# Three groups of small TensorE products per attention head placed beside other small groups, and the weight-sum jobs of GpSimd in another order

## What is computed

```python
def diff_attn_core(q, k, v, q_pos, k_pos, lam):
    s = jnp.einsum('bqhmd,bkhmd->bhmqk', q, k).astype(jnp.float32) * (DIFF_HEAD_DIM ** -0.5)
    visible = (k_pos[None, :] // CHUNK) <= (q_pos[:, None] // CHUNK)
    p = jax.nn.softmax(jnp.where(visible, s, NEG), axis=-1)
    a = p[:, :, 0] - lam * p[:, :, 1]
    return jnp.einsum('bhqk,bkhe->bqhe', a.astype(v.dtype), v)

def finish_layer(x, a, b, ga, gb, w_a, w_b, w_o, g1, b1, w_up, w_down, g2, b2):
    mix = (ga * (a @ w_a) + gb * (b @ w_b)) @ w_o
    x = layer_norm(ALPHA * x + mix, g1, b1)
    h = jnp.square(jax.nn.relu(x @ w_up)) @ w_down
    return layer_norm(ALPHA * x + h, g2, b2)
```

## Time and profile before

| | us |
|---|---|
| median of 3 runs | 2132.62 (2132.21 to 2136.03) |
| profiled execution, time | 2132.67 |
| profiled execution, span of the core | 2130.9 |
| PE busy | 2116.2 |
| DVE / ACT busy | 1472.1 / 1230.6 |
| HBM over the span | 228 GB/s |

### The profile page before, as it was taken

One profiled execution on the slowest core, in us unless ns is written; L12 is line 12 of the kernel. 1 busy time (PEld: TensorE's weight loads), 2 busy tenths in 40 slices (PEclk: granted clock), 3 DMA queues, 4 the chain that ended last, 5 costly groups with the idle time before them and its releaser, 6 DMA issues.

```text
span 2130.9 us, 38215 instructions
## 1 busy us (share of the span) xinstructions
PE 2116.2 (99%) x15004; PEld 1935.2 (91%) x15004; DVE 1472.1 (69%) x2336; ACT 1230.6 (58%) x2493; POOL 64.6 (3%) x100
## 2 busy tenths in 40 slices
PE   9999999999999999999999999999999999999998
PEld 8998889999989898989889888899999898989897
DVE  6857777766879356665667577786778793566656
ACT  4457776696535356656234577766965353556561
POOL 1000000001000000000001000000110001000000
PEclk9999999999999999999999999999999999999999
DMA  7887562487861855454368765524778527544541
GB/s 251 237 291 257 204 219 107 146 250 218 222 228 50 237 158 171 146 168 139 109 188 240 279 251 211 211 79 156 244 206 246 204 73 224 166 165 154 168 149 70
DMA packets 100867, 399.27 MB, mean 187 GB/s; under 512 B 15273, under 2 KB 16937, under 8 KB 87601
## 3 DMA queue, kind: packets, MB, share of 16 engines
q1 hardware_dynamic: 67904, 191.55, 26.4%
q0 software_dynamic: 7936, 92.28, 17.1%
q10 hardware_dynamic: 24848, 112.99, 14.8%
HBM read 367.42 MB, written 118.23 MB: 228 GB/s over the span
## 4 chain that ended last, share of the span: by engine, by line
PE 96%; DMA 2%; ACT 1%; DVE 1%; issue 0%; ACTq 0%; DVEq 0%
PE PS L828 9%; PE PS L830 9%; PE PS L829 9%; PE PS L1049 6%; PE PS L1051 6%; PE PS L1050 6%; PE PS L917 5%; PE PS L919 5%; PE PS L918 5%; PE PS L863 4%; PE PS L862 4%; PE PS L861 4%; PE PS L987 3%; PE PS L988 3%; PE PS L989 3%; PE PS L1177 2%
## 5 line engine op out<-in xcount | busy, mean ns | idle before, releaser
L828 PE MATMUL PS<-xt_hi,w_hi 128*128 128x320 f32 x1184 | 382.3, 323 | 0.2
L830 PE MATMUL PS<-xt_hi,w_lo 128*128 128x320 f32 x1184 | 365.9, 309 | 0.0
L829 PE MATMUL PS<-xt_lo,w_hi 128*128 128x320 f32 x1184 | 365.7, 309 | 0.0
L2541 DVE TENSOR_TENSOR w_lo<-w_raw,w_hi 128x1024 fp32r<-128x1024 f32 x146 | 177.5, 1222 | 151.0 <-ACT w_hi L1579 149.4
L2548 DVE TENSOR_TENSOR w_lo<-w_raw,w_hi 128x1024 fp32r<-128x1024 f32 (+1 forms) x176 | 199.3, 1138 | 114.8 <-ACT w_hi L1595 114.5
L1579 ACT ACTIVATE w_hi<-w_raw 128x1024 fp32r<-128x1024 f32 x146 | 153.6, 1059 | 178.5 <-PE PS L1051 152.6
L828 PEld LDWEIGHTS PS<-xt_hi,w_hi 128*128 128x128 f32 x1184 | 222.8, 188 | 5.4 <-issue 4.3
L829 PEld LDWEIGHTS PS<-xt_lo,w_hi 128*128 128x128 f32 x1184 | 223.0, 188 | 0.1
L830 PEld LDWEIGHTS PS<-xt_hi,w_lo 128*128 128x128 f32 x1184 | 222.3, 188 | 0.0
L1595 ACT ACTIVATE w_hi<-w_raw 128x1024 fp32r<-128x1024 f32 (+1 forms) x176 | 172.2, 984 | 86.1 <-PE PS L989 66.3
L1049 PE MATMUL PS<-w_hi,act_a_hi 128*128 128x512 f32 x480 | 187.9, 391 | 2.3 <-DVE rows L3007 2.3
(11 more groups left out here) (391 smaller groups left out, 5095.0 us busy)
## 6 DMA issues: line engine op xcount, KB each, us to landing
w_raw<-in_weights SPq DMA_DIRECT2D x186, 512.0 KB, 4.8
kc<-in_k_cache ACTq DMA_DIRECT2D x32, 1024.0 KB, 7.7
vc<-in_v_cache ACTq DMA_DIRECT2D x16, 2048.0 KB, 8.7
w_raw<-up_sums SPq DMA_DIRECT2D x112, 256.0 KB, 2.9
up_sums<-in_up_blocks POOLq DMA_DIRECT2D x24, 1024.0 KB, 9.0
w_raw<-in_up_blocks SPq DMA_DIRECT2D x84, 256.0 KB, 2.8
down_sums<-in_down_blocks POOLq DMA_DIRECT2D x16, 1024.0 KB, 11.3
w_raw<-in_down_blocks SPq DMA_DIRECT2D x32, 512.0 KB, 3.4
```

Source lines behind the costliest of these rows:

```text
L828: mm(out, wh, hi[:, k, c], start=(k == 0), stop=False)
L829: mm(out, wh, lo[:, k, c], start=False, stop=False)
L830: last = mm(out, wl, hi[:, k, c], start=False, stop=(k == KT - 1))
L2541: v.tensor_tensor(w_lo[slot][:], raw[:, raw_of(s, n)[0], :], w_hi[slot][:].bitcast(F32), ALU.subtract)\
```

## The change

```diff
 def sum_jobs():
 
-    return [(l, kind, part) for l in range(DEPTH) for part in range(FF_PARTS) for kind in ("up", "down")
-            if kind == "up" or part in BLOCK_PARTS]
+    order = (("up", 1), ("down", 1), ("up", 0), ("up", 2), ("down", 2), ("up", 3))
+    return [(l, kind, part) for l in range(DEPTH) for kind, part in order]
...
             for j, (l, kind, part) in enumerate(SUM_JOBS):
-                if (kind, part) == ("up", 0):
+                if (kind, part) == ("up", 1):
                     pool.wait_ge(w_ready[0], nth(l, AT_V) + 1)
-                elif (kind, part) == ("down", 1):
+                elif (kind, part) == ("up", 0):
                     pool.wait_ge(swa_cache_loaded, 32 * (l + 1))
...
-                tile(0, 0, None if first else {(0, 1): lambda: unit_transpose(l, h - 1, (3,)),
+                tile(0, 0, None if first else {(0, 1): lambda: (unit_product(l, h - 1, (2,)),
+                                                                unit_transpose(l, h - 1, (3,))),
                                                (0, 6): lambda: mean_squares(n - 1)})
...
                 if not first:
                     output_transposes(l, h - 1, 7)
-                tile(1, 0, {(0, 2): lambda: dec_transposes(l, h, 0), (0, 5): lambda: dec_transposes(l, h, 1)})
+                dec_transposes(l, h, 0)
+                tile(1, 0, {(0, 4): lambda: dec_transposes(l, h, 1)})
                 dec_products(l, h)
                 unit_score(l, h, p, (3,))
                 unit_transpose(l, h, (0, 1))
-                tile(1, 1, {(1, 4): lambda: dec_map_sum(l, h),
-                            (1, 5): lambda: (unit_product(l, h, (0, 1)), unit_transpose(l, h, (2,)))})
-                unit_product(l, h, (2,))
+                tile(1, 1, {(1, 5): lambda: (unit_product(l, h, (0, 1)), dec_map_sum(l, h),
+                                             unit_transpose(l, h, (2,)))})
 
             def last_head_end(l):
-                early_gate(l, 2, 0, {(0, 1): lambda: unit_transpose(l, HEADS - 1, (3,)),
+                early_gate(l, 2, 0, {(0, 1): lambda: (unit_product(l, HEADS - 1, (2,)),
+                                                      unit_transpose(l, HEADS - 1, (3,))),
                                      (0, 6): lambda: mean_squares(l * HEADS + HEADS - 1)})
```

## The result

| | before | after |
|---|---|---|
| median of 4 runs, us | 2132.41 (2131.74 to 2136.03) | 2153.49 (2150.72 to 2155.11) |
| profiled execution, time / span, us | 2132.67 / 2130.9 | 2153.41 / 2151.6 |
| granted TensorE clock over the span | 0.999 | 0.995 |

The ratio is 1.0094 (95% interval 1.0075 to 1.0114): slower, by 21 us. I had forecast +9.6 us, 2142.3, with 2150 as the high end. The direction was right, the size was not, and the time lies outside the range.

A forecast was written before the change was run, and what follows sets the result against it. PE was taken as the bound, busy 2116.2 of 2130.9 us. The terms -1.3 + 8.4 + 1.3 + 3.5 - 2.3 = +9.6 us, on 2132.67, gave 2142.3 us, range 2137 to 2150.

The forecast's parts named there:

- The stall: Heads 1 to 7, both layers: fifth decode transpose waits for ACT's copy out of bank 7; 14 x 0.60 = +8.4 us.
- The rival in which the wait does not bite: Heads: ACT copies sooner or the fifth transpose is not held; +1.2, 2133.9 us, no change; chance 0.06.
- Grouping: PE in all 16 heads: putting small groups together saves 0.08 us a head, -1.3 us, between 0 and -2.
- The end of the last head: Early gate 2: unit 2's six products no longer cover the wait for gate 1's copy; +0.66 a layer, +1.3 us.
- The O stage: Waits before L1049 vanish because POOL's last transfer goes out some 15 us earlier; -2.3 us, between -2.3 and 0.
- The keys: Head 0's cached-key loads delayed by POOL transfers: +3 in layer 1, +0.5 in layer 0; +3.5 us, -1.8 to +11.
- The rival of crowding: V and gates: weights come late beside two large jobs, +5.7 to +11.4 us on top, 2148 to 2154; chance 0.12.
- costly borders: PE drains at each small-group border, 48 groups freed; at 0.35 us each the change is faster, 2126.8; chance 0.04.
- good luck with both transfers: O-stage and key-load transfer terms both go well, -2.3 and -1.8, stall as forecast: +4.3, 2137.0 us; chance 0.10.

The follow-up runs named there:

- experiment 3: Original kernel with only the decode transposes of the regrouping, moved right behind the output transposes: 2139.51 us, ratio 1.0039.
- experiment 5: Original kernel with the change's PE moves, but the fifth transpose and the second transpose group in their old places, old job order: 2131.07 us, ratio 1.0004.
- experiment 4: Original kernel with only the map sum and unit 2 product moved, that product in its old place in the last head: 2128.91 us, ratio 0.9992.
- experiment 2: Original kernel with only the three regrouped products on PE, weight sums in the old order: 2139.67 us, ratio 1.0039.
- experiment 1: Original kernel with only the new order of the weight-sum jobs on POOL, PE as before: 2143.52 us, ratio 1.0052.
- experiment 6: Original kernel with the new job order, but down 1 held until the keys of each layer's second head landed: 2127.14 us; again 2127.67; both ratio 0.9986.
- experiment 7: Original kernel with the new job order and throwaway matmuls before the waits for head 0's keys: 2140.03 us, ratio 1.0043.
- experiment 9: Original kernel with the new job order, down 1 held back, plus the map sum and unit 2 product moves: 2126.03 us, ratio 0.9978.
- experiment 8: Original kernel with jobs in the order up 1, up 0, then down 1, up 2, down 2, up 3: 2128.23 us, ratio 0.9993.

## Why the prediction was right and wrong

- **The stall: right.** Forecast 0.60 us in 14 heads, +8.4. The timeline shows 0.59, experiment 3 gives 0.66 between heads (+9.2), experiment 5 takes it away. The signs named for it came: 14 gaps of 0.43 us, and 28.1 us from head to head. The rival in which the wait does not bite falls.
- **Grouping: a size off.** Forecast -1.3. The change's head is 0.62 longer where the transposes alone make 0.66, and experiment 4 gives 0.04 a head: -0.6. I had taken 0.06 for `dec_map_sum`, the upper end of its bounds; the lower was nearer.
- **The end of the last head: right.** +1.3 forecast, +1.3 measured.
- **The O stage: right, roughly.** -2.3 forecast, -2.8 measured. The wait of L1049 is itself loose: with the old order it was 2.3 in the rows of before, 0.9, 3.4 and 2.0 in experiments 2, 3 and 4, and absent in experiment 5. With the new order it is absent in every trace (after, experiments 1, 6, 7 and 9, and the second one of 6); in experiment 8, whose third job is again a large one, it is 1.3.
- **The keys: here the prediction failed.** The step reads "I take +3 in layer 1 and +0.5 in layer 0 ...: +3.5". Measured is +13.4, of it 4.14 + 3.38 = 7.5 in waits and 5.9 at half clock; the order alone (experiment 1) makes it and holding back one job (experiment 6) removes it. Three things were off. The wait of layer 0 was charged at 0.5, because that load had no wait before; but its slack, 2.8 us, was never worked out. The trace of before has the first job start at 18.87 us there, and with 52 + 57.5 us of jobs my own figures put the second one's end at about 128, beyond the load's issue at 117 to 119. It ended at 139.8. The delay of the loads themselves was inside my bounds of 0 to 10 us (the second half took 15.6 instead of 8.5 in layer 0, 17.5 instead of 13.3 in layer 1); what it costs PE was not worked out from it. In layer 1 the waits were 5.2 us where the forecast has 1.8 + 3 = 4.8, but that is partly luck: POOL's second job landed at 1213.3 with PE 9.7 us later than before, so at 1203.6 on the forecast's scale, outside its 1178 to 1199. The two jobs took 60 and 66 us there, and I had taken 52 and 60. And the clock was not in the sum at all: I priced a wait by its length only, and the 1.8 us wait of before, behind which the clock was full, said nothing of longer ones.
- **The rival of crowding** had the right cause and the wrong place: no weight came late in V or gates; it was `kc` in head 0, in both layers. Its 2148 to 2154 holds the measured time by a cause that it didn't name. The other two rivals, costly borders and good luck with both transfers, did not come.

What stays open: why the lateness falls now on the first half of the keys, now on the second (2.89 us in experiment 7, 6.87 in experiment 1), and so why layer 0 costs 6.6 in one trace and 9.9 in another. Nor is it explained how long the half clock lasts: the two traces with 5.2 and 5.5 us of waits in layer 1 had 10.2 and 6.8 us of it.

## What to carry to other kernels

Before moving a small group, list every semaphore that it waits for with the slack at its old place: one instruction, the fifth transpose, had 0.35 us of it and was moved up by 0.94, and with that one kept back (and the group behind it) the time stayed. When background transfers are reordered, compare the *end* of each job with the issue of the next load that has no time to spare, layer by layer; a job held until the next head's load had landed, too, cost nothing here. And in a stream that keeps TensorE full, price a wait of some microseconds at its length plus what follows at half clock, here 0.4 to 0.65 of the wait again.

## What the runs showed of the hardware

- Waits of 1.8 to 2.0 us in a full PE stream (before, experiments 2, 3 and 4) left the clock at 2.4 GHz. One of 2.89 us came with 3.4 us at 1.2 GHz (experiment 7), one of 4.14 with 6.8 (after), and one of 6.87 with 10.2 (experiment 1). Two of 2.45 and 2.75 us, with 1.85 us of matmuls between, came with 10.2 (after), and two of 3.55 and 1.97, with 1.07 between, with 6.8 (experiment 1). The loss beyond the waits was 2.4 to 3.4 us in each layer of after and of experiment 1.
- 14 stalls of 0.6 us, one in 28 us, left it full.
- Throwaway matmuls in the waits held the clock at full in layer 1 of experiment 7, and gave back 2.2 us.
- A small float32 group between large matmuls of the same 128*128 form costs next to nothing for its borders: moving two groups a head together gave 0.04 us (experiment 4).
- 1 MB transfers of POOL beside ACT's loads took 35.0% of the DMA engines' time to ACT's 38.5%, where it had been 9.5 to 64.6, from 112 to 138 us of the span, and the longest landing of `kc` grew from 13.3 to 17.5 us (18.5 in experiment 1, 19.7 in experiment 7).
